# Second output product of a two-layer diffusion trunk: products 1 and 2 first, block by block, and the fifth group of modulation columns turned behind the first combined tile

## What is computed

```python
for l in range(DEPTH):                       # DEPTH = 2
    mp = modulation(c_ctx[None, :], ada_w[l], ada_b[l])   # six parts
    ms = modulation(c, ada_w[l], ada_b[l])
    ...
    if l % 2 == 0:
        ...                                  # y = concat(o_mla, o_ret) @ w_out
    else:                                    # conformer_conv
        u = depthwise_conv(a * sigmoid(g), dw, dw_b)
        u = layer_norm(u, ln_g, ln_b)
        y = silu(u) @ w_out
    x = x + m[2] * y
    h = modulate(rms_norm(x, norm_ffn[l]), m[3], m[4])
    x = x + m[5] * hier_moe(h, ...)
```

## Time and profile before

| | us |
|---|---|
| median of three runs | 1319.2 |
| lowest and highest of them | 1317.21, 1320.07 |
| the profiled execution's own time | 1319.7 |
| its span in the profile | 1317.9 |
| PE busy | 1185.1 |
| DVE, ACT, POOL busy | 606.3, 380.9, 434.0 |

### The profile page before, as it was taken

The page is one execution under the profiler, slowest core; times in us unless marked ns, Lnnn a source line. Parts: engine busy times, 40 slices in busy tenths (PEclk is TensorE's granted clock), DMA queues, the critical chain, the costliest instruction groups (busy, mean ns, idle before and its releaser), DMA issues.

```text
span 1317.9 us, 20755 instructions
## 1 busy us (share of the span) xinstructions
PE 1185.1 (90%) x6709; PEld 746.4 (57%) x6710; DVE 606.3 (46%) x1381; ACT 380.9 (29%) x786; POOL 434.0 (33%) x739
## 2 busy tenths in 40 slices
PE   6999998989999499997786799999799599999884
PEld 5566797555566455553342666666377355555442
DVE  3120344776866522221110739999785422222226
ACT  2120036655522211111110436565514111111111
POOL 0300100340000134443332449997600234444420
PEclk9999999979999799999997899999899799999997
DMA  9775550000053899999997921111763899999976
GB/s 378 267 287 215 210 178 33 3 1 1 1 101 148 349 394 422 423 423 423 424 423 302 301 81 64 64 64 33 196 203 150 316 375 397 384 422 423 422 284 271
DMA packets 107301, 324.76 MB, mean 246 GB/s; under 512 B 23029, under 2 KB 56795, under 8 KB 84707
## 3 DMA queue, kind: packets, MB, share of 16 engines
q1 hardware_dynamic: 86640, 290.38, 57.1%
q0 software_dynamic: 12464, 21.91, 4.7%
q10 hardware_dynamic: 8131, 11.59, 2.5%
HBM read 314.53 MB, written 27.11 MB: 259 GB/s over the span
## 4 chain that ended last, share of the span: by engine, by line
PE 59%; issue 14%; DVE 8%; DMA 7%; POOL 6%; ACT 2%; SPq 2%; POOLq 1%; ACTq 1%; DVEq 0%
PE PS L1270 10%; PE PS L806 9%; PE PS L762 9%; PE PS L1127 8%; PE PS L1149 4%; PE PS L996 3%; POOL arena L2536 2%; PE PS L695 2%; DMA arena<-in_moe_w_down 2%; DVE arena L1754 2%; DMA arena<-in_moe_w_up 2%; DMA ring<-in_ada_w 2%; PE PS L1112 2%; DVE scratch L1754 2%; PE PS L1009 1%
## 5 line engine op out<-in xcount | busy, mean ns | idle before, releaser
L1754 DVE TENSOR_TENSOR arena<-arena,PS 128x128 f32<-128x128 f32 (+3 forms) x109 | 40.2, 385 | 288.8 <-ACT arena L1645 287.6
L1270 PE MATMUL PS<-arena,ring 128*128 128x320 f32 x512 | 141.8, 438 | 7.8 <-issue 6.5
L1127 PE MATMUL PS<-ring,arena 128*64 128x256 f32 x1088 | 131.2, 393 | 16.4 <-DMA ring<-in_moe_w_up 14.7
L2623 POOL TENSOR_TENSOR arena<-arena 128x655 f32<-128x655 f32 x91 | 129.7, 1425 | 42.8 <-ACT arena L1717 30.0
L806 PE MATMUL PS<-ring,arena 128*128 128x256 f32 (+1 forms) x640 | 141.9, 375 | 1.7 <-ACT arena L1457 1.7
L1127 PE MATMUL PS<-arena 128*64 128x256 f32 x1120 | 130.6, 383 | 13.9 <-DMA arena<-in_moe_w_up 12.8
L806 PEld LDWEIGHTS PS<-ring,arena 128*128 128x128 f32 x640 | 115.6, 192 | 28.8 <-issue 14.5
L762 PE MATMUL PS<-arena,ring 128*128 128x320 f32 x448 | 123.8, 439 | 5.1 <-ACT arena L1732 4.8
L1270 PEld LDWEIGHTS PS<-arena,ring 128*128 128x128 f32 x512 | 98.0, 193 | 51.3 <-issue 12.7
L2355 DVE SCALAR_TENSOR_TENSOR PS<-arena,vecT,PS 128x655 f32<-128x655 f32 x124 | 112.1, 904 | 4.2
L1127 PEld LDWEIGHTS PS<-ring,arena 128*64 128x64 f32 x1088 | 77.9, 140 | 59.4 <-DMA ring<-in_moe_w_up 13.3
(11 more groups left out here) (363 smaller groups left out, 1613.7 us busy)
## 6 DMA issues: line engine op xcount, KB each, us to landing
arena<-in_moe_w_up SPq DMA_DIRECT2D x64, 1024.0 KB, 19.2
ring<-in_moe_w_up SPq DMA_DIRECT2D x64, 1024.0 KB, 15.0
ring<-in_ada_w SPq DMA_DIRECT2D x46, 1024.0 KB, 10.9
arena<-in_moe_w_down SPq DMA_DIRECT2D x32, 1024.0 KB, 20.0
ring<-in_moe_w_down SPq DMA_DIRECT2D x32, 1024.0 KB, 16.3
arena<-y_rows ACTq DMA_DIRECT2D x10, 1024.0 KB, 9.5
ring<-in_od_w_in SPq DMA_DIRECT2D x16, 512.0 KB, 6.2
ring<-in_ev_w_in SPq DMA_DIRECT2D x7, 1024.0 KB, 15.8
```

The source lines that it names most:

```text
L1127: last = pe.matmul(PS[i * BLK:(i + 1) * BLK, 0, 0:2 * P].rearrange("p (a n) -> p a n", a=2), xblk[:, k, :], w[:, k % 4, :, i * P:(i + 1) * P],
L1270: last = pe.matmul(PS[:, 2 * a + n, 0:SEG], w[:, k, a, :], hT[:, k, n * SEG:(n + 1) * SEG], start=(k == 0), stop=(k == KD - 1))
L1754: return dve.tensor_tensor(out, a, b, op)
L2623: pool.tensor_tensor(acc, acc, prod[:, i % PRODS, :], ALU.add).then_inc(ev("conv_p"), 1)
```

## The change

In the second output product (layer 1) product 2 goes before product 5, in both passes. In its first pass products 1 and 2 go block by block: block i of the first tile, then block i of the second, before block i + 1. The wait for `mod_c` goes from product 2 to product 5, whose groups now use banks 5 and 7. Layer 0's order stays. `last_sum` still waits for product 2, whose step is now earlier. At the end of layer 0's experts `mod_columns(4)` and PE's wait for the bias come behind `combine(0)`, and DVE's `mod_bias(4)` behind `residual(0)`.

```diff
@@ build @@
-        ORDER = (1, 5, 2, 6, 3, 7, 4)
+        ORDERS = ((1, 5, 2, 6, 3, 7, 4), (1, 2, 5, 6, 3, 7, 4))
...
-        def out_step(mt, product):
+        def out_step(l, mt, product):
 
-            return 14 * (mt // 2) + 2 * ORDER.index(product) + mt % 2 + 1
+            return 14 * (mt // 2) + 2 * ORDERS[l].index(product) + mt % 2 + 1
...
@@ project_out, ready @@
-                    elif product == 2:
+                    elif product == 5:
                         pe.wait_ge(ev("mod_c"), MODC + 6)
@@ project_out @@
-                    for product in ORDER:
-                        for mt in (2 * q, 2 * q + 1):
+                    for product in ORDERS[l]:
+                        pair = (2 * q, 2 * q + 1)
+                        for mt in pair:
                             ready(mt, product)
+                        by_chunk = l == 1 and q == 0 and product in (1, 2)
+                        for n in range(8):
+                            mt, i = (pair[n % 2], n // 2) if by_chunk else (pair[n // 4], n % 4)
                             c = slice(mt % 2 * P, mt % 2 * P + P)
-                            for i in range(4):
-                                if l == 1 and mt == 0 and product in (1, 2):
-                                    pe.wait_ge(ev("ln_sq"), KD + 1 + (0 if product == 1 else 4) + i + 1)
...
+                            if l == 1 and mt == 0 and product in (1, 2):
+                                pe.wait_ge(ev("ln_sq"), KD + 1 + (0 if product == 1 else 4) + i + 1)
...
-                            last.then_inc(ev("wo_mm"), 1)
+                            if i == 3:
+                                last.then_inc(ev("wo_mm"), 1)
@@ tensor, moe @@
                     for n in range(4 * KD, 5 * KD):
                         modulation(n)
-                    mod_columns(4)
-                    pe.wait_ge(ev("mod_c"), MODC + 5)
...
                 for s in range(NT + 2):
                     if s < NT:
                         combine(s)
+                    if s == 0:
+                        mod_columns(4)
+                        pe.wait_ge(ev("mod_c"), MODC + 5)
                     if s >= 2:
                         tile_sum(s - 2)
@@ vector, moe @@
                     gate_block(n)
-                if l == 0:
-                    mod_bias(4)
-
...
                 for s in range(NT + 3):
                     if s < NT:
                         residual(s)
+                    if s == 0:
+                        mod_bias(4)
@@ gpsimd, last_sum @@
-                pool.wait_ge(ev("wo_mm"), 28 * l + out_step(2 * q + 1, 2))
+                pool.wait_ge(ev("wo_mm"), 28 * l + out_step(l, 2 * q + 1, 2))
```

More of the change, by code:

```diff
@@ L440, in build, with out_bank @@
                 3: ((0, 1),), 7: ((4, 0), (4, 1)), 4: ((4, 0),)}
-        def out_step(mt, product):
-            return 14 * (mt // 2) + 2 * ORDER.index(product) + mt % 2 + 1
-        def out_bank(mt, product):
-            return (1, 4, 3, 6, 5, 7)[(out_step(mt, product) - 1) % 6]
+        def out_step(l, mt, product):
+            return 14 * (mt // 2) + 2 * ORDERS[l].index(product) + mt % 2 + 1
+        def out_bank(l, mt, product):
+            return (1, 4, 3, 6, 5, 7)[(out_step(l, mt, product) - 1) % 6]
         def row_done(l, k):
-            return 28 * l + out_step(k % 4, 3 if k < 4 else 4)
+            return 28 * l + out_step(l, k % 4, 3 if k < 4 else 4)
         back_full = {}
@@ L726, in ready @@
                     q = mt // 2
-                    if out_step(mt, product) > 6:
-                        pe.wait_ge(ev("wo_ev"), n0 + out_step(mt, product) - 6)
+                    if out_step(l, mt, product) > 6:
+                        pe.wait_ge(ev("wo_ev"), n0 + out_step(l, mt, product) - 6)
                     if product in (5, 6, 7):
@@ L763, in project_out @@
-                            last.then_inc(ev("wo_mm"), 1)
+                            if l == 1 and mt == 0 and product in (1, 2):
+                                pe.wait_ge(ev("ln_sq"), KD + 1 + (0 if product == 1 else 4) + i + 1)
+                            left = {1: w1[:, K1[l] + i, c], 2: w1[:, K2[l] + i, c], 3: w1[:, K2[l] + i, c],
+                                    4: w2[:, K2[l] + i, c], 5: weight_sum(l, q, 0)[:, i, c],
+                                    6: weight_sum(l, q, 1)[:, i, c], 7: w2[:, K1[l] + i, c]}[product]
@@ L765, in _ @@
+                            right = {1: x1(i)[:, 0:SEG], 2: x2(i)[:, 0:SEG], 3: x2(i)[:, SEG:T], 4: row_sum[:, 3, i, :],
+                                     5: row_sum[:, 0, i, :], 6: row_sum[:, 1, i, :], 7: row_sum[:, 2, i, :]}[product]
+                            last = pe.matmul(PS[:, out_bank(l, mt, product), 0:SEG], left, right, start=(i == 0), stop=(i == 3))
+                            if i == 3:
+                                last.then_inc(ev("wo_mm"), 1)
             pe.wait_ge(ev("params_in"), 16 * NPARAM)
@@ L2072, in take @@
                 def take(mt, product):
-                    dve.wait_ge(ev("wo_mm"), 28 * l + out_step(mt, product))
+                    dve.wait_ge(ev("wo_mm"), 28 * l + out_step(l, mt, product))
                     if product != 1:
-                        dve.wait_ge(ev("wo_ev"), 28 * l + out_step(mt, product) - 2)
+                        dve.wait_ge(ev("wo_ev"), 28 * l + out_step(l, mt, product) - 2)
                     for row, n in USES[product]:
@@ L2080, in take @@
                             last = dve.scalar_tensor_tensor(
-                                out=xT[:, m, c0:c1], in0=PS[:, out_bank(mt, product), c0 - n * SEG:c1 - n * SEG],
+                                out=xT[:, m, c0:c1], in0=PS[:, out_bank(l, mt, product), c0 - n * SEG:c1 - n * SEG],
                                 scalar=modT[:, l, 16 + m, who:who + 1], in1=xT[:, m, c0:c1], op0=ALU.mult, op1=ALU.add)
```

## The result

The changed kernel's median is 1327.55 us (1326.13 to 1329.70, five runs) against 1319.20 (1317.21 to 1320.37, five runs): a ratio of 1.0063, 95% interval 1.0046 to 1.0080, so 8.4 us slower. The forecast had the direction and three of its mechanisms, but not the size: 1324.4, at most 1326.8.

A forecast was written before the change was run, and what follows sets the result against it. PE was taken to bound the kernel. Columns +1.6, order +1.9 and clock +1.7 made +5.2 us on the profiled 1319.7, so 1324.9, or 1324.4 against the 1319.2 median; range 1319.6 to 1326.8.

The forecast's parts named there:

- What bounds the kernel: Whole kernel: PE is busy 90% of the span; a PE delay in the combine or second output product delays all that follows.
- Part 1, the columns: End of layer 0's experts: moved columns make PE wait for DVE's bias behind the first combined tile, +1.6 us.
- The load's 6.9 us: First combined tile: its rows land 6.9 us after the load's issue at 714.11, so it cannot start before 721.0.
- the margin of 1.25 us behind the bias: First combined tile, before the change: PE starts 1.25 us after the bias is done, waiting for the load.
- Part 2, the order: Second output product, layer 1: the new order delays PE's seventh group, +1.9 us, bounds -0.5 and +2.6.
- The gap of 0.48 us: Behind product 1: product 2 needs no row sum, so PE starts it 0.48 us earlier; half lost again, -0.2.
- block by block: First two products of the second output product: ACT's blocks are always ahead of PE, so another block order is worth nothing.
- POOL's turn: Layer 1 row sums: POOL's earlier last difference runs 2.21 us before DVE's fourth sum, which ends 2.16 us later.
- Rival (b): Row sums: DVE's fourth sum goes before POOL's waiting instruction; together +1.4 us, 1320.6, within 0.2%; chance 0.25.
- The step that failed: Second output product: PE's seventh group waits for the first group's evictions, starting at 961.7 in place of 959.83, +1.9 us.
- Part 3, the clock: Behind PE's 2.2 us stall: clock falls to 1.2 GHz for 3.4 us, costing +1.7 us, bounds 0 and 3.4.
- The Trainium skill's rule: POOL against DVE's row sums: two-SBUF-input DVE and SBUF-reading GpSimd instructions block each other whole, issue order deciding; same +1.9.

The follow-up runs named there:

- experiment 11: Kernel before with the columns moved behind the first combined tile, PE waiting for their bias only before the half tile using their bank; last combine record at 20.4 us, one execution.
- experiment 7: Kernel of experiment 5, but layer 1's DVE evicts products 1 and 2 between two pairs of row sums, POOL's second-pass weight sums last; ratio 0.9995, 1317.6 us.
- experiment 9: Kernel before with only eight unread matmuls filling PE's idle time before product 1 of the second output product; ratio 1.0009, 1320.8 us.
- experiment 5: Changed kernel with PE's waits apart again, POOL's last layer 1 differences behind the row sums, columns ahead of the combined tiles; ratio 0.9992, 1317.5 us.
- experiment 1: Changed kernel with PE's wait for each group of four matmuls right before that group again, not both tiles' waits before the pair; ratio 1.0032, 1323.9 us.
- experiment 2: Changed kernel with the modulation columns and their bias back ahead of the first combined tile, new product order kept; ratio 1.0048, 1325.0 us.
- experiment 6: Kernel before with only PE's waits for both tiles of a product taken before the pair's first matmul, in both layers; ratio 1.0015, 1320.3 us.
- experiment 4: Changed kernel, but POOL's last weight differences in layer 1 wait for DVE's four row sums; ratio 1.0025, 1324.0 us.
- experiment 8: Kernel of experiment 7 plus eight unread matmuls filling PE's idle time before product 1 of the second output product; ratio 0.9966, 1314.4 us.
- experiment 10: Kernel of experiment 8 plus ten unread matmuls ahead of the convolution module's first product; ratio 0.9964, 1314.7 us.
- experiment 12: Kernel of experiment 10, but layer 1's router weights are loaded from SP's queue and not ACT's; ratio 0.9963, 1313.9 us.

## Why the prediction was wrong, point by point

**What bounds the kernel** was right: PE's delay in the second output product passed to the end. Of the stage's 7.1 us nothing that a trace can tell came back, with 310.5 and 310.1 us behind it (308.8 to 312.5 over all profiles).

**Part 1, the columns: +1.6** was right. Measured +1.5 at the place, and 1.6 between the two groups of profiles; experiment 11 gives the split. The load's 6.9 us was that one profile's, and the margin of 1.25 us behind the bias with it: in six of the eight other profiles without the move PE starts its first tile 0.35 to 0.6 us behind the bias, and in experiments 7 and 9 only 0.06 us, so there the bias came last. The load was the gate as said, but barely.

**Part 2, the order.** The gap of 0.48 us went, and block by block was worth nothing, as said (experiment 5: 63.2 us against 63.4, where -0.2 was forecast). POOL's turn was right in mechanism and size: the sum of 959.11 took 3.63 us, where 959.54 - 955.90 = 3.64 was worked out. POOL's waiting instruction did go before DVE's next one. Rival (b), which had DVE's fourth sum first, is refuted by every run with the early difference (experiments 1 and 2).

**The step that failed** is in part 2: "PE's seventh group starts at 961.7 in place of 959.83", with "the eighth needs the second eviction (963.7) and comes at 963.9 anyway". It held the waits to be where they were before, one tile at a time. The changed loop takes both ahead of the pair, so the seventh group too waits for the second eviction: it starts 4.2 us later than before, where +1.9 was said and +2.6 was the bound. Experiment 1 undoes that one line and gives the prediction's own stage, 67.0 us; experiment 6 has that line alone and costs 2.2 us.

**Part 3, the clock: +1.7** was right for a gap of 2.2 us: experiments 1 and 4 have gaps of 2.06 us and low stretches of 3.4 us. With the gap at 4.3 us it was 6.8 us of low clock and 2.9 us lost, 1.2 more. That the longer stretch comes of the longer gap, and so of the same failed step, is likely and not shown: other gaps (last section) gave either length. So the sum was short by 2.3 of stall and 1.2 of clock: 1324.4 + 3.5 = 1327.9, measured 1327.55. That it agrees to 0.4 us is in part luck, since the five runs lie between 1326.13 and 1329.70.

**The Trainium skill's rule** (SBUF — State Buffer, Who interferes with whom) of an exclusive turn in the order of issue holds for the case on which the forecast rested: POOL asked at 958.81 us, DVE's fourth sum started at 959.11, and POOL went first, 2.58 us with its wait for the third sum. The near tie of experiment 9 doesn't show it: there DVE's record starts 0.01 us ahead of POOL's and DVE waited.

## What to carry to other kernels

When a loop is rewritten so that two chains of work interleave, look at where its waits went. A wait that moves ahead of a pair costs as much as the later chain's producer is behind, also in the iterations that were not interleaved (layer 0, where PE never waited, lost nothing). And when an engine's step is released earlier, ask what it now runs beside: POOL's 2.4 us, harmless beside the evictions, cost 2.2 us in the middle of DVE's two-operand sums. In a stage that PE bounds, filling the idle time ahead of it kept the clock up and was worth more than the whole reordering. Whether it needs DVE's early evictions too is not settled: without them (experiment 9) it gained nothing, but that profile had its lost turn.

## What the runs showed that was not expected

A tie decides 2.2 us. In the stage's start DVE issues a 128x8 instruction with two SBUF operands at the same moment as POOL issues a weight sum, while POOL's previous one is still finishing. In nine of the ten profiles in which both meet, the kernel before and the changed one among them, the two start within 0.01 us of each other and DVE goes first, 0.15 us. In the tenth (experiment 9), with the same 0.01 us between them, it lost and took 2.37 us, and PE's gap and a low clock followed. Since it needs no other cause than 0.01 us, some of the spread between executions of one kernel (1315 to 1325 us over the runs of the kernel before in one session) may come from there; that is not shown. The kernels of experiments 7, 8, 10 and 12 hold POOL back and have no such meeting.

The clock after a single gap in the second output product, PE being busy on both sides: 1.92 us left it alone (experiment 6), 2.06 lowered it for 3.4 us (experiments 1 and 4), 4.3 and 4.8 for 6.8 us (the changed kernel, experiment 2). The length of the low stretch does not follow from the gap alone. Every profile has a gap of 4.4 us near 220 us, with the same work on both sides. Behind it the clock was low for 3.4 us in twelve of the fourteen profiles and for 6.8 us in two (experiments 5 and 6). The changed kernel's gap, with the clock back at 1.00 from 226 us on, then experiment 5's, with 0.50 for the whole of 218 to 224:
```profile
221.67 0.52 PE L882 MATMUL PS<-cst,arena 128*128 128x128 f32 x3 [4.37 <-DVE arena L1926]
226.00:229.00 3.00, 3.00 (x17) 2.63 (x16) 0.81 (x3) 1.51 (x8) 0.00 (x0) 1.00 0.00 0
...
218.40 0.87 PE L882 MATMUL PS<-cst,arena 128*128 128x128 f32 x3 [4.37 <-DVE arena L1925]
218.00:224.00 6.00, 5.60 (x15) 4.60 (x16) 2.23 (x9) 1.68 (x9) 0.00 (x0) 0.50 0.01 3
```
So the clock's share of a loss that was read from one profile, 2.9 us in the changed kernel, can be another in its next execution.
